# Expert rows summed in DRAM by accumulating scatters, tiles finished under the last two experts, weights loaded in pairs of pieces

## The reference

```
xn2 = rmsnorm(x1)                                  # x1: residual stream, 1280 x 1024
group = argmax(4 group logits); e1, e2 = top 2 of the 8 experts in the group
w1, w2 = softmax(top two logits) * softmax(group logits)[group]
for each (token, expert):  y = (silu(xn2 @ w_gate[e]) * (xn2 @ w_up[e])) @ w_down[e]
out = rmsnorm(x1 + w1 * y_e1 + w2 * y_e2)
```

## Time and profile before

| | |
|---|---|
| median of 3 runs | 1171.67 us (1170.9 to 1173.81) |
| the profiled execution | 1169.87 us, of which the span of the trace is 1168.1 us |
| busy: TensorE, VectorE, ScalarE, GpSimd | 98%, 73%, 60%, 23% |
| bytes moved by DMA | 324.11 MB, of which q1 279.18 MB and q0 44.27 MB |
| the experts' steps | about 566 to 1129 us |
| after the last product | 1129 to 1168 us |

### The profile page before, as it was taken

The page is one execution under the profiler, slowest core; times in us unless marked ns, Lnnn a source line. Parts: engine busy times, 40 slices in busy tenths (PEclk is TensorE's granted clock), DMA queues, the critical chain, the costliest instruction groups (busy, mean ns, idle before and its releaser), DMA issues.

```text
span 1168.1 us, 18708 instructions
## 1 busy us (share of the span) xinstructions
PE 1142.5 (98%) x5934; PEld 962.9 (82%) x5934; DVE 857.4 (73%) x1340; ACT 699.1 (60%) x1134; POOL 273.3 (23%) x348
## 2 busy tenths in 40 slices
PE   8999999999999999999999999999999999999987
PEld 8988888888889888887888888888888888888863
DVE  6649510134437766677899999999999999999957
ACT  6342241233438744334788787787887887887834
POOL 2200210001200012223142332332332325443320
PEclk9999999999999999999999999999999999999999
DMA  7312240446969644444999999999999999999989
GB/s 223 90 36 83 90 136 1 128 144 220 312 242 365 219 139 157 155 176 157 390 407 388 396 386 401 381 399 386 388 385 393 387 386 392 379 398 388 381 253 359
DMA packets 137795, 324.11 MB, mean 277 GB/s; under 512 B 25526, under 2 KB 62304, under 8 KB 137744
## 3 DMA queue, kind: packets, MB, share of 16 engines
q1 hardware_dynamic: 120032, 279.18, 65.1%
q0 software_dynamic: 17712, 44.27, 10.5%
HBM read 285.37 MB, written 51.12 MB: 288 GB/s over the span
## 4 chain that ended last, share of the span: by engine, by line
PE 63%; DMA 25%; DVE 6%; issue 3%; ACT 2%; SPq 0%; ACTq 0%; DVEq 0%; POOLq 0%
DMA e_st<-in_expert_w_down_dram 19%; PE psum L937 17%; PE psum L939 17%; PE psum L938 17%; DVE e_lo L2037 3%; DMA units<-mlstm_units 1%; PE psum L1127 1%; ACT e_hi L1533 1%; DMA e_st<-in_expert_w_gate_dram 1%; PE psum L1221 1%; PE psum L951 1%; PE psum L1062 1%; DMA e_st<-in_expert_w_up_dram 1%; PE psum L1063 1%; PE psum L1299 1%
## 5 line engine op out<-in xcount | busy, mean ns | idle before, releaser
L2037 DVE TENSOR_TENSOR e_lo<-e_st,e_hi 128x1024 fp32r<-128x1024 f32 x384 | 447.0, 1217 | 26.4 <-ACT e_hi L1533 25.6
L1533 ACT ACTIVATE e_hi<-e_st 128x1024 fp32r<-128x1024 f32 x384 | 388.3, 1056 | 50.8 <-DMA e_st<-in_expert_w_down_dram 35.1
L939 PE MATMUL psum<-e_hi,ex_lo 128*128 128x512 f32 x512 | 199.5, 390 | 0.0
L937 PE MATMUL psum<-e_hi,ex_hi 128*128 128x512 f32 x512 | 199.4, 389 | 0.0
L938 PE MATMUL psum<-e_lo,ex_hi 128*128 128x512 f32 x512 | 199.2, 389 | 0.0
L937 PE MATMUL psum<-xT_hi,w_hi 128*128 128x512 f32 (+1 forms) x432 | 151.1, 350 | 2.2 <-DVE w_lo L1673 1.4
L939 PE MATMUL psum<-xT_hi,w_lo 128*128 128x512 f32 (+1 forms) x432 | 149.4, 346 | 0.0
L938 PE MATMUL psum<-xT_lo,w_hi 128*128 128x512 f32 (+1 forms) x432 | 149.2, 345 | 0.0
L858 POOL COPY row_to<-rows_to 128x1 int32 (+1 forms) x30 | 46.6, 1554 | 295.2 <-DVE yo L2119 295.2
L937 PEld LDWEIGHTS psum<-e_hi,ex_hi 128*128 128x128 f32 x512 | 96.1, 188 | 20.2 <-DVE ex_lo L2108 0.2
L939 PEld LDWEIGHTS psum<-e_hi,ex_lo 128*128 128x128 f32 x512 | 96.1, 188 | 20.0
(11 more groups left out here) (292 smaller groups left out, 1857.2 us busy)
## 6 DMA issues: line engine op xcount, KB each, us to landing
e_st<-in_expert_w_gate_dram SPq DMA_DIRECT2D x128, 512.0 KB, 13.6
e_st<-in_expert_w_up_dram SPq DMA_DIRECT2D x128, 512.0 KB, 13.7
e_st<-in_expert_w_down_dram SPq DMA_DIRECT2D x128, 512.0 KB, 14.5
mlstm_units<-stage SPq DMA_DIRECT2D x18, 640.0 KB, 3.9
w_st<-in_w_in_dram SPq DMA_DIRECT2D x20, 512.0 KB, 4.4
xn_scratch<-xn POOLq DMA_DIRECT2D x20, 512.0 KB, 3.9
stage<-gate_rows SPq DMA_DIRECT2D x18, 512.0 KB, 5.8
e_st<-expert_rows SPq DMA_DIRECT2D x15, 512.0 KB, 10.0
```

The source lines that it names most:

```text
L937: pe.matmul(out, a_hi, b_hi, start=start, stop=False)
L939: return pe.matmul(out, a_lo, b_hi, start=False, stop=stop)
L1533: act.activation(e_hi[:, r, :, :], e_st[:, slot, :, :], ACT.Copy).then_inc(ehi_done, 1)
L2037: dve.tensor_tensor(e_lo[:, r, :, :], e_st[:, slot, :, :], e_hi[:, r, :, :].bitcast(F32), ALU.subtract).then_inc(elo_done, 1)
```

## The change

**Sums in DRAM.** expert_rows is replaced by row_sums (1280 x 1024). As each tile's x1 is ready, before the experts, GpSimd stores it there (10 DMAs of 512 KB). Each step's scatter goes to the row of the token and adds (compute_op=ADD); GpSimd works out the token numbers (tokens_to) once with two operations. The swapping in route_rest goes, and four small VectorE operations on the weights with it.

**The end.** Once the scatters of all but the last two steps have landed, SyncE loads the ten tiles of sums into x1 and they are squared, scaled and stored, all without the rows of the last two experts. For these two, "late 0" and "late 1", GpSimd gathers the sums of their tokens into gx, VectorE adds the product out of PSUM (late_total), and the rows are normed and scattered over the stored outputs, once all ten stores have landed: two indirect DMAs for each, to y_sample and to y_prompt. The accumulating loads, the second loads, the sums on VectorE and TensorE and TensorE's keep-warm matmuls go. The last down product uses banks 0 and 1.

**Weights.** Two pieces come in one DMA of 1 MB with 8 KB to a partition (pair_in). It is issued when both slots are free, and hi_part waits for the whole pair. The order of pieces becomes gate, gate, up, up; TensorE's work on a piece stays.

```diff
-    y_dram = nc.dram_tensor("expert_rows", (2 * T, D), F32).ap()
+    sum_dram = nc.dram_tensor("row_sums", (T, D), F32).ap()
...
+    TAIL = [0, 1, 2, 3, "late 0", 8, 9, 4, "late 1", 5, 6, 7]
+    TAIL_AT = {x: n for n, x in enumerate(TAIL)}
...
-            def piece_in(piece, src, d2):
+            def pair_in(piece, src):
                 number, slot, _, _ = piece
-                wait(sp, elo_done, number - NST + 1)
-                dst = e_st[:, slot, :, :]
-                sp.dma_start(dst if d2 else dst.rearrange("p a n -> p (a n)"), src).then_inc(e_load[slot], 16)
+                wait(sp, elo_done, number + 2 - NST)
+                sp.dma_start(e_st[:, slot:slot + 2, :, :].rearrange("p s a n -> p (s a n)"), src).then_inc(e_load[slot], 16)
 
             def gu_in(i, c):
-                w = expert_w_up if c % 2 else expert_w_gate
-                kk = 2 * (c // 2)
-                piece_in(gu_piece(i, c), w[0, bass.ds(expert_at(i), 1), :, :]
-                         .rearrange("a (p k) n -> p (a k) n", k=KD)[:, kk:kk + 2, :], True)
+                w = expert_w_up if c // 2 % 2 else expert_w_gate
+                kk = 4 * (c // 4)
+                pair_in(gu_piece(i, c), w[0, bass.ds(expert_at(i), 1), :, :]
+                        .rearrange("a (p k) n -> p (a k) n", k=KD)[:, kk:kk + 4, :].rearrange("p k n -> p (k n)"))
 
             def down_in(piece, e, c):
-                piece_in(piece, expert_w_down[0, bass.ds(expert_at(e), 1), :, :]
-                         .rearrange("a (p k) n -> p (a k) n", k=KF)[:, c, :], False)
+                pair_in(piece, expert_w_down[0, bass.ds(expert_at(e), 1), :, :]
+                        .rearrange("a (p k) n -> p (a k) n", k=KF)[:, c:c + 2, :].rearrange("p k n -> p (k n)"))
...
             sp.wait_ge(elo_done, down_piece(last, 3)[0] + 1)
             for b in range(2):
-                sp.wait_ge(y_out[b], 16 * n_half - 32)
-            for t in range(N_ADDED, NT):
-                slot = early_slot(t)
-                sp.dma_start(spare(slot), y_dram[t * P:(t + 1) * P, :]).then_inc(e_load[slot], 16)
-            for b in range(2):
-                sp.wait_ge(y_out[b], 16 * n_half)
-            for t in LATE_ORDER:
-                slot = late_slot(t)
-                if slot < NT - N_ADDED:
-                    sp.wait_ge(f_sum, slot + 1)
-                sp.dma_start(spare(slot), y_dram[T + t * P:T + (t + 1) * P, :]).then_inc(e_load[slot], 16)
-            for t in range(NT):
-                sp.wait_ge(f_done, t + 1)
-                sp.dma_start(tokens(t, y_prompt, y_sample), x1[:, t, :]).then_inc(f_out, 16)
+                sp.wait_ge(y_out[b], 16 * n_half - 16)
+            for t in (0, 1, 2, 3, 8, 9, 4, 5, 6, 7):
+                sp.dma_start(x1[:, t, :], sum_dram[t * P:(t + 1) * P, :]).then_inc(e_load[t] if t < 8 else sum_load[t - 8], 16)
+            for t in TAIL:
+                if t in range(NT):
+                    sp.wait_ge(f_done, TAIL_AT[t] + 1)
+                    sp.dma_start(tokens(t, y_prompt, y_sample), x1[:, t, :]).then_inc(f_out, 16)
             sp.wait_ge(f_out, 16 * NT)
+            sp.wait_ge(late_out, 16 * 4)
...
+                        in_=rowval[:, k, order[i]:order[i] + 1], in_offset=None).then_inc(list_out[i % 2], 16)
 
             for i, t in enumerate(order):
+                pool.wait_ge(x1_done, i + 1 if i < NT - 1 else NT + 1)
+                pool.dma_start(sum_dram[t * P:(t + 1) * P, :], x1[:, t, :]).then_inc(sums_out, 16)
...
+
+                pool.tensor_copy(token_of[:, b:b + 1], tokens_to[:, bass.ds(i, 1)]).then_inc(row_placed, 1)
+                pool.wait_ge(row_placed, i + 1)
+                pool.sem_inc(pool_past, 1)
+
             def rows_out(i, b):
                 pool.wait_ge(y_left, i + 1)
                 pool.wait_ge(y_right, i + 1)
-                pool.tensor_copy(row_to[:, b:b + 1], rows_to[:, bass.ds(i, 1)]).then_inc(row_placed, 1)
-                pool.wait_ge(row_placed, i + 1)
-                pool.sem_inc(pool_past, 1)
+                token_rows(i, b)
                 pool.indirect_dma_start(
-                    out=y_dram, out_offset=bass.IndirectOffsetOnAxis(ap=row_to[:, b:b + 1], axis=0),
-                    in_=yo[:, b, :], in_offset=None, bounds_check=2 * T - 1, oob_is_err=False).then_inc(y_out[b], 16)
+                    out=sum_dram, out_offset=bass.IndirectOffsetOnAxis(ap=token_of[:, b:b + 1], axis=0),
+                    in_=yo[:, b, :], in_offset=None, bounds_check=T - 1, oob_is_err=False,
+                    compute_op=ALU.add).then_inc(y_out[b], 16)
 
...
+            pool.tensor_scalar(tokens_to[:, :], rows_to[:, 0:NT * E], T, -T, ALU.is_ge, ALU.mult).then_inc(pool_step, 1)
+            pool.wait_ge(pool_step, 21)
+            pool.tensor_tensor(tokens_to[:, :], tokens_to[:, :], rows_to[:, 0:NT * E], ALU.add).then_inc(pool_step, 1)
+            pool.wait_ge(pool_step, 22)
+            pool.wait_ge(sums_out, 16 * NT)
...
                 weights_in(2 * j + 2, 0)
             for b in range(2):
-                pool.wait_ge(y_out[b], 16 * n_half - 32)
-                pool.sem_inc(pool_past, 1)
-            for t in range(N_ADDED):
-                add_rows(t)
-            for b in range(2):
                 pool.wait_ge(y_out[b], 16 * n_half - 16)
                 pool.sem_inc(pool_past, 1)
             for b in range(2):
-                pool.tensor_copy(row_to[:, b:b + 1],
-                                 rows_to[:, bass.ds(2 * n_half - 2 + b, 1)]).then_inc(row_placed, 1)
+                pool.tensor_copy(token_of[:, b:b + 1],
+                                 tokens_to[:, bass.ds(2 * n_half - 2 + b, 1)]).then_inc(row_placed, 1)
             pool.wait_ge(row_placed, 2 * n_half)
             pool.sem_inc(pool_past, 1)
+            pool.wait_ge(ext_ready, 4 * n_half + 2)
+            pool.sem_inc(pool_past, 1)
             for b in range(2):
-                pool.wait_ge(y_left, 2 * n_half - 1 + b)
-                pool.sem_inc(pool_past, 1)
-                pool.wait_ge(y_right, 2 * n_half - 1 + b)
-                pool.sem_inc(pool_past, 1)
                 pool.indirect_dma_start(
-                    out=y_dram, out_offset=bass.IndirectOffsetOnAxis(ap=row_to[:, b:b + 1], axis=0),
-                    in_=yo[:, b, :], in_offset=None, bounds_check=2 * T - 1, oob_is_err=False).then_inc(y_out[b], 16)
+                    out=gx[:, b, :], out_offset=None, in_=sum_dram,
+                    in_offset=bass.IndirectOffsetOnAxis(ap=token_of[:, b:b + 1], axis=0),
+                    bounds_check=T - 1, oob_is_err=False).then_inc(late_load[b], 16)
+            pool.tensor_scalar(late_far[:, :], token_of[:, :], S0, 4 * T, ALU.is_lt, ALU.mult).then_inc(pool_step, 1)
+            pool.tensor_scalar(late_to[:, :], token_of[:, :], -S0, None, ALU.add).then_inc(pool_step, 1)
+            pool.wait_ge(pool_step, 24)
+            pool.tensor_tensor(late_to[:, :], late_to[:, :], late_far[:, :], ALU.add).then_inc(pool_step, 1)
+            pool.wait_ge(pool_step, 25)
+            pool.wait_ge(f_out, 16 * NT)
+            for b in range(2):
+                pool.wait_ge(f_done, TAIL_AT[f"late {b}"] + 1)
+                pool.indirect_dma_start(
+                    out=y_sample[0, :, :], out_offset=bass.IndirectOffsetOnAxis(ap=late_to[:, b:b + 1], axis=0),
+                    in_=yo[:, b, :], in_offset=None, bounds_check=S1 - 1, oob_is_err=False).then_inc(late_out, 16)
+                pool.indirect_dma_start(
+                    out=y_prompt[0, :, :], out_offset=bass.IndirectOffsetOnAxis(ap=token_of[:, b:b + 1], axis=0),
+                    in_=yo[:, b, :], in_offset=None, bounds_check=S0 - 1, oob_is_err=False).then_inc(late_out, 16)
 
...
                                         (e_hi[:, r, kk, :], e_lo[:, r, kk, :]), k == 0, k == KD - 1)
                     last.then_inc(piece_used, 1)
 
-            def down(piece, i, b, turned=None):
+            def down(piece, i, b, turned=None, bank=4):
 
                 pe.wait_ge(htlo_done, i + 1)
-                wait(pe, y_left, i)
-                wait(pe, y_right, i)
...
+                act.wait_ge(e_load[slot - slot % 2], 16 * loads)
                 wait(act, piece_used, number - NRG + 1)
                 act.activation(e_hi[:, r, :, :], e_st[:, slot, :, :], ACT.Copy).then_inc(ehi_done, 1)
...
+            def root(x):
+                n = TAIL_AT[x]
+                if x in range(NT):
+                    if x < 8:
+                        act.wait_ge(e_load[x], 16 if x % 2 else 16 * (last_i + 2))
+                    else:
+                        act.wait_ge(sum_load[x - 8], 16)
+                    total, ss, rms = x1[:, x, :].rearrange("p (a n) -> p a n", a=2), wts[:, 2, x:x + 1], wts[:, 3, x:x + 1]
+                else:
+                    k = int(x == "late 1")
+                    act.wait_ge(late_sum, k + 1)
+                    total, ss, rms = yo[:, k, :].rearrange("p (a n) -> p a n", a=2), stat[:, 0, k:k + 1], stat[:, 1, k:k + 1]
```

(72 more changed lines are left out.)

129 lines of the change are left out of this document (27 added, 102 removed).

## The result

The changed kernel took 1191.91 us (median; 1187.55 to 1192.65), the kernel before 1172.74 beside it: ratio 1.0162, 95% interval 1.0134 to 1.0190. That is slower by 19 us, and above the range. The profiled execution took 1191.47 us. Of the runs further down, one execution of plain_single (4980 us) and one of acc_80 (1665 us) were far slower than the others; the ratios leave them out, and they move the two medians by less than 0.3 us.

A forecast was written before the change was run, and what follows sets the result against it. The prediction took the DMA engines, a little over TensorE's 17.77 us a step, to bound the loop. Scatters +22.4, long rows -15.9 and pairs +1.0 gave +7.5; with the end's -8.9, 1171.67 went to 1170.3 us, range 1158 to 1187.

The forecast's parts named there:

- What bounds the loop: Expert loop: DMA engines need a little over TensorE's 17.77 us a step; added packets cost at once.
- the clock stays up: TensorE in the loop: rival had the clock falling every step, 30 steps some 50 us longer, about 1220; chance 0.03.
- 30 x 0.324 x 36.8 / 16 = 22.4: Loop's 30 accumulating scatters: extra packet time shared by all 16 engines, 22.4 us, 0.75 a step; bounds 0 and 44.8.
- another such reading time: Loop's scatters: rival that accumulating into DRAM costs more than into SBUF, another 22.4 us, 1192.7; chance 0.10.
- It saves 768 x 9.5 ns: Loop's weight loads: rows of 8 KB halve the large packets, 0.46 us a step; with small packets 15.9 us over 31 steps.
- The rival that such rows are cut: Loop's weight loads: 8 KB rows travel as 4 KB packets and save only 1.8 us, 1184.4; chance 0.20.
- Pairs 1.0: Loop's weight loads: issuing and waiting by pairs shortens the lead, costing 1.0 us, bounds 0 and 3.0.
- The end, -8.9: After the loop: last weights, sums, stores and four late scatters end 8.9 us sooner, bounds 6 and 11.
- What was hidden: Before and beside the experts: stores of x1 (13 us uncovered), tokens_to and copies of token_of covered by waiting.

The follow-up runs named there:

- plain_single: Changed kernel with plain scatters (sums not formed) and single 512 KB weight DMAs with 4 KB rows, the new end kept: 1164.24 us, ratio to before 0.9935.
- acc_80: Changed kernel with each accumulating scatter over the first 80 places of its list, 142 of 2389 rows left out: 1164.60 us, ratio to before 0.9961.
- thin: Changed kernel loading only 64 KB in place of 1 MB for every weight pair after the first six: 1163.11 us, one execution.
- acc_direct: Changed kernel with each scatter replaced by a direct accumulating store of 80 rows into row_sums, without a list: 1166.91 us, ratio to before 0.9962.
- spread: Changed kernel in full, an expert's rows placed over all 128 partitions of its list from the second expert on: 1201.76 us, ratio to before 1.0251.
- after: The changed kernel itself, with the full change against the kernel before: 1191.91 us, ratio to before 1.0162.
- double_out: Changed kernel with each accumulating scatter as two plain scatters, to row_sums and a second array: 1193.27 us, ratio to before 1.0180.
- plain: Changed kernel with its 30 scatters as plain writes to row_sums, sums not formed: 1164.26 us, ratio to before 0.9944.
- acc_sbuf: Changed kernel with each scatter replaced by an accumulating direct load of 80 rows from DRAM into SBUF: 1177.27 us, ratio to before 1.0040.
- plain_load: Changed kernel with plain scatters and, beside each, a plain direct load of 80 rows from DRAM into x1: 1195.76 us, ratio to before 1.0215.
- direct_two: Changed kernel with each scatter replaced by a plain direct store and a plain direct load of 80 rows, no list: 1186.87 us, ratio to before 1.0129.
- twice: Changed kernel with each weight pair as two 512 KB DMAs with 4 KB rows, issued and waited for together: 1202.56 us, ratio to before 1.0267.
- lists_first: Changed kernel with the row lists asked for before pair 6, 7 of the first expert's weights: 1192.74 us, ratio to before 1.0186.
- acc_96: Changed kernel with each accumulating scatter over the first 96 places of its list, 11 rows left out: 1166.27 us, ratio to before 0.9957.
- acc_112: Changed kernel with each accumulating scatter over the first 112 places of its list, no rows left out: 1176.81 us, ratio to before 1.0044.
- before_pairs: Kernel before with only the loading of weights in pairs (1 MB, rows of 8 KB) added: 1167.91 us, ratio to before 0.9967.

## Why the prediction was wrong, point by point

**What bounds the loop: right.** The DMA engines do (thin), of them those with the most rows (below), and each added microsecond showed. That the clock stays up was right too.

**"30 x 0.324 x 36.8 / 16 = 22.4": the step that failed.** The price for a MB was right: an accumulated row of 4 KB takes 327 ns, a plain one 159. The division by 16 was wrong: it takes the rows as spread evenly over the 16 engines, and they are not. In a list of 128 places, the 80 or so rows in use are 8 on each of eight engines. Those eight get 8 x (0.327 - 0.159) = 1.34 us more a step, not 0.75, 40 us in 30 steps. Measured were 35.1 us with single pieces and, with pairs, whose plain form leaves the engines some slack beside TensorE, 27.6. With the rows spread evenly accumulation costs next to nothing: 2.7 us for all of them directly (acc_direct), nothing that can be measured for 94% of them in lists of 80 places (acc_80). The upper bound, "another such reading time" for 44.8 us, held the size, but that rival's chance was 0.10 for want of a row, and the number came out by another mechanism.

**How the rows are shared out: shown in thin.** There the DMA engines are mostly free (share 0.28 from 640 to 1000 us), and the start and length of each packet can be read from the trace. A scatter's unused places (its packets of 8 bytes) give the rows in use, 128 less their number. The packets of rows in progress 0.2 to 0.5 us after the first then say how many engines have rows:

| rows in use | 59, 64 | 66, 67 | 69 to 72 | 74 to 76 | 82 to 84 | 86 | 90 to 92 | 93 to 103 |
|---|---|---|---|---|---|---|---|---|
| packets of rows at once | 8 | 9 | 10 | 11 | 13 | 14 | 15 | 16 |

28 of the 30 scatters are in it; the first shows 5 and the last 13. 2.7 to 3.3 us after the first packet about 8 are still in progress in nearly all of them (10 with 103 rows), the engines with most rows. Blocks of 8 neighbouring places would give 11 for 82 rows and 12 for 92. The Trainium skill ("DMA: Bandwidth & Descriptors", "The descriptor swizzle") says which partitions an engine has: groups of four partitions in turn over engines 0 to 7 for partitions 0 to 63, over 8 to 15 for the others. By that rule 80 rows at the front are 8 on each of eight engines, 4 on four and none on four; every column of the table agrees with it. The order of spread also puts 8 on each of eight engines by that rule. Then spread did not test what it was meant to, and its result agrees with the rule.

In the full loop the same shows in how long a scatter's row packets go on, from the first to the last: 5.1 us in after and 5.2 in spread, 4.5 with 112 places, 4.2 with 96, 3.7 with 80 and 3.3 in acc_direct (medians, 740 to 1080 us).

**What it costs: an estimate from the packets' medians.** On the busiest engine a step has 48 weight packets of 8 KB at 0.309 us, 8 gathered rows at 0.159, and the scattered rows; small packets are left out of the estimate. In after that is 14.83 + 1.27 + 8 x 0.327 = 18.72 us, measured 18.83. With 7, 6 and 5 scattered rows, an even share of 112, 96 and 80 places, it is 18.39, 18.06 and 17.74, measured 18.41, 18.03 and 17.80. double_out comes to 18.65 (18.87); plain to 17.38, under TensorE's 17.77; the kernel before, with 96 packets of 4 KB, to 17.81 (17.89). acc_direct comes to 17.74 (17.76). The runs with a direct load into SBUF do not fit: acc_sbuf 17.74 (18.08), plain_load 18.17 (19.05), direct_two 17.69 (18.86).

A price for each unused place is the rival. From 128 to 112 places, 30 x 16 = 480 fewer, 15.1 us went, 0.5 us of one engine for each. By it the 48 more in a step of double_out than of after would add 1.5 us, and they add nothing; it would have to be a price of accumulating places alone, and in thin their packets take 8 ns. An order that puts 5 rows on each engine in a list of 128 would settle the rest, and was not run.

DMA share and GB/s in 40 slices of 800 to 840 us, and the scatters there (start us, us), first of after:

```profile
DMA  9999999999999999699989999999999799969979
GB/s 332 320 320 352 365 369 418 410 430 418 438 385 320 369 426 352 229 410 393 344 311 348 365 377 352 406 414 430 446 410 311 320 410 393 279 262 442 344 242 320
```

```profile
815.52 1.68 POOL L831 DMA_INDIRECT row_sums<-yo,token_of  x1 [0.90 <-POOL token_of L823]
...
833.75 1.75 POOL L831 DMA_INDIRECT row_sums<-yo,token_of  x1 [0.88 <-POOL token_of L823]
```

and of acc_direct:

```profile
DMA  9999999989999999999999999999999999999999
```

In after some engines stand still for a while (the 6 at 816 us, the 7 at 831, the 6 at 835), and not while the unused places are moved: their packets begin at 819.3 and 838.0, and a scatter has landed 10.6 us after its issue. Packet by packet, 13 or fewer are in progress for 5.1% of the time from 740 to 1080 us, for 3.3% with 112 places, 1.0% with 96, 0.4% with 80 and 0.1% in acc_direct. It fits engines with few rows that run out of weights while those with many are behind. In plain it is 3.2% and costs nothing, as TensorE sets the step there.

**"It saves 768 x 9.5 ns", 15.9 us: too large.** 10.7 (twice beside after), which is 6.4 ns a packet, inside the bounds. The rival that such rows are cut was wrong: weight rows went as packets of 8192 bytes. The Trainium skill ("DMA: Bandwidth & Descriptors", "SWDGE vs HWDGE vs iDMA") prefers packets of at most 4096 bytes; going past it cost nothing here.

**"Pairs 1.0": 3.2**, just over its upper bound.

**The end, -8.9: right,** -7.7. The gain is real and alone is worth 0.65%; the stretch from the first late scatter to the end was 3 us longer than I took.

**What was hidden** was hidden: stores of x1, tokens_to, the row lists (lists_first).

## What to carry to other kernels

A transfer with a list of row numbers takes as long as the engine that has the most of its rows. Before dividing its bytes by 16, count the rows on the busiest engine: in a list of 128 with the rows in use at the front that was 8 here, with 60 rows as with 100. A list cut to the rows in use spreads them (acc_96, acc_80; here the longest expert, 103 rows, sets how far one may go). The gathers have the same lists of 128 in all these kernels and were not cut. When the DMA engines are full, a new kind of transfer is priced by one run in its place, not by the packet times of another kind. And split a change: here the end and the pairs were each worth having, one addition cost more than both.

## What the runs showed of the hardware

- A place of a list that is out of bounds is a packet of 4 bytes, or 8 when accumulating (867 of these in 340 us of after, 616 in acc_112, 297 in acc_96, none in acc_direct). In a quiet queue it takes 8 ns (thin).
- In a list of 128 places with the rows in use at the front, 59 to 64 rows are moved by 8 of the engines, 82 to 84 by 13, 93 and more by all 16, and the busiest have 8 rows each (thin).
- An accumulating row of 4 KB takes two plain rows' packet time (327 ns for 159), but accumulating directly into DRAM, 80 rows a time, made the kernel only 2.7 us longer for 9.8 MB.
- An accumulating direct load of 80 rows out of DRAM in each step costs 10.4 us more in the whole kernel than an accumulating direct store of as many (1177.3 beside 1166.9).
- Rows of 8 KB save next to nothing where TensorE sets the step (389 GB/s before, 391 in before_pairs, 740 to 1080 us), and 10.7 us where the DMA engines do.
